# A rebuilt opening for a two-block transformer kernel: x by column halves, the first norm from token rows, weight tiles split one by one

## What is computed

```python
h = rmsnorm(x, norm1[l])        # x*rsqrt(mean(x*x)+1e-6) * gain
proj = h @ w_in[l]              # 1024 -> N_IN; q, k, v of two mixers and the gates
```

## Time and profile before

| | |
|---|---|
| runs, median (lowest to highest) | 2931.31 us (2926.85 to 2935.4) |
| the profiled execution: its time, its span | 2937.29 us, 2935.5 us |
| PE matmul busy | 2825.1 us (96% of the span) |
| PE weight loads busy | 2310.7 us (79%) |
| DVE busy | 1600.3 us (55%) |
| ACT busy | 1122.4 us (38%) |
| POOL busy | 33.6 us (1%) |
| mean granted TensorE clock | 0.984 of 2.4 GHz |
| HBM traffic | 85 GB/s over the span |

### The profile page before, as it was taken

The page is one execution under the profiler, slowest core; times in us unless marked ns, Lnnn a source line. Parts: engine busy times, 40 slices in busy tenths (PEclk is TensorE's granted clock), DMA queues, the critical chain, the costliest instruction groups (busy, mean ns, idle before and its releaser), DMA issues.

```text
span 2935.5 us, 34699 instructions
## 1 busy us (share of the span) xinstructions
PE 2825.1 (96%) x13232; PEld 2310.7 (79%) x13232; DVE 1600.3 (55%) x2164; ACT 1122.4 (38%) x1536; POOL 33.6 (1%) x36
## 2 busy tenths in 40 slices
PE   5999989999999999999999999999999899999998
PEld 4898778888879877788887887888878568788886
DVE  5358665545644866553666655434563445644444
ACT  2126534423412553442343344322442644533222
POOL 2000000000020000000000000000000000000000
PEclk8999999999999999999999999999999999999999
DMA  3322132233322113233324323333232113233322
GB/s 98 105 64 58 58 86 86 86 102 93 106 86 87 44 47 97 72 93 108 96 85 119 91 79 108 93 107 89 86 98 74 29 44 108 65 100 93 102 81 83
DMA packets 467506, 249.91 MB, mean 85 GB/s; under 512 B 21238, under 2 KB 463439, under 8 KB 467279
## 3 DMA queue, kind: packets, MB, share of 16 engines
q1 hardware_dynamic: 467407, 248.54, 29.0%
HBM read 246.41 MB, written 2.10 MB: 85 GB/s over the span
## 4 chain that ended last, share of the span: by engine, by line
PE 88%; DVE 6%; ACT 3%; issue 1%; DMA 1%; SPq 0%; DVEq 0%; ACTq 0%
PE M L655 25%; PE M L656 24%; PE M L657 24%; DVE w_lo L1862 2%; PE M L728 1%; PE M L729 1%; PE M L730 1%; PE A L848 1%; PE A L785 1%; PE A L816 1%; PE A L860 1%; ACT w_hi L1324 1%; PE A L829 0%; PE A L801 0%; PE A L655 0%
## 5 line engine op out<-in xcount | busy, mean ns | idle before, releaser
L655 PE MATMUL M<-h_hi,w_hi 128*128 128x512 f32 x2264 | 893.7, 395 | 10.2 <-DVE w_lo L1862 9.9
L656 PE MATMUL M<-h_lo,w_hi 128*128 128x512 f32 x2264 | 884.2, 391 | 0.0
L657 PE MATMUL M<-h_hi,w_lo 128*128 128x512 f32 x2264 | 884.0, 390 | 0.0
L1324 ACT ACTIVATE w_hi<-stage 128x1024 fp32r<-128x1024 f32 (+3 forms) x516 | 504.3, 1020 | 758.5 <-PE M L657 647.4
L1862 DVE TENSOR_TENSOR w_lo<-stage,w_hi 128x1024 fp32r<-128x1024 f32 (+3 forms) x516 | 610.9, 1222 | 135.7 <-ACT w_hi L1324 134.8
L655 PEld LDWEIGHTS M<-h_hi,w_hi 128*128 128x128 f32 x2264 | 426.7, 188 | 106.1 <-issue 14.4
L656 PEld LDWEIGHTS M<-h_lo,w_hi 128*128 128x128 f32 x2264 | 426.7, 188 | 90.5 <-issue 2.9
L657 PEld LDWEIGHTS M<-h_hi,w_lo 128*128 128x128 f32 x2264 | 426.4, 188 | 89.9
L655 PE MATMUL M<-hid_hi,w_hi 128*128 128x512 f32 x704 | 274.6, 390 | 6.9 <-DVE hid_lo L1996 6.9
L656 PE MATMUL M<-hid_lo,w_hi 128*128 128x512 f32 x704 | 273.9, 389 | 0.0
L657 PE MATMUL M<-hid_hi,w_lo 128*128 128x512 f32 x704 | 273.9, 389 | 0.0
(11 more groups left out here) (417 smaller groups left out, 3351.5 us busy)
## 6 DMA issues: line engine op xcount, KB each, us to landing
stage<-in_w_up SPq DMA_DIRECT2D x88, 512.0 KB, 4.2
stage<-in_ffn_w_gate_up SPq DMA_DIRECT2D x88, 512.0 KB, 3.8
stage<-in_w_in SPq DMA_DIRECT2D x80, 512.0 KB, 3.7
stage<-in_w_down SPq DMA_DIRECT2D x32, 384.0 KB, 3.5
stage<-in_ffn_w_down SPq DMA_DIRECT2D x32, 384.0 KB, 3.5
stage<-in_od_w_in SPq DMA_DIRECT2D x21, 512.0 KB, 3.9
stage<-in_w_down SPq DMA_DIRECT2D x32, 320.0 KB, 3.5
stage<-in_ffn_w_down SPq DMA_DIRECT2D x32, 320.0 KB, 3.3
```

Source lines behind the costliest of these rows:

```text
L655: pe.matmul(bank, a_hi, b_hi, start=(n == 0), stop=False)
L656: pe.matmul(bank, a_hi, b_lo, start=False, stop=False)
L657: last = pe.matmul(bank, a_lo, b_hi, start=False, stop=(n == k - 1))
L1324: act.activation(w_hi[:, s, part * HALF:part * HALF + n], stage[:, part, 0:n], ACT.Copy)\
```

## The change

Line numbers after it are those of the changed kernel. What it does:

- SP's order is now: columns 0 to 511 of x for all tokens (1 MB), the identity (64 KB), `norm1` (16 rows), weight tile 0, columns 512 to 1023 of x (1 MB), weight tile 1, the rest of row group 0, then tile 2 when `w_lo_done` is 1, group 1, tile 3 when it is 2, the other constants, groups 2 and 3 and the gate bias.
- PE turns tile 0, `norm1` alone (L909, into M[1]), tiles 1 to 3, waits for the second half of x, and turns 4 to 7. The tiles go to six banks (`turn_bank`), so only tiles 6 and 7 wait for a bank.
- ACT and DVE make `h_hi` (L1620) and `h_lo` (L2257) directly from the turned banks; DVE copies them to `x` (L2262) in between.
- The four tiles of chunks 0 and 1 are split one by one (L1615, L2251); PE takes a tile (24 matmuls, L681 to L683) when that tile is split.
- The sum of squares comes from ACT over token rows (`Square` with accumulation, L1631), 4 of 128x1024; `rstd_col` is made from it (L1634, L1636), and PE spreads it to `rstd` by 4 transposes (L934) after chunk 0, which ACT copies (L1639). DVE's 8 additions and PE's sums are gone.
- The rest of `vec` is turned after chunk 1 (L946) and read after DVE has split chunk 3 (L2305).

```diff
-            sp.dma_start(const[:, 0:C_BIAS], dram["shape_constants"][:, 0:C_BIAS]).then_inc(tokens_landed, 16)
-            for j in range(TT):
-                sp.dma_start(x_tok[:, j, :], dram["x"][0, j * P:(j + 1) * P, :]).then_inc(tokens_landed, 16)
...
+            sp.dma_start(x_tok[:, :, 0:half], x_rows[:, :, 0:half]).then_inc(tokens_landed, 16)
+            sp.dma_start(const[:, 0:P], dram["shape_constants"][:, 0:P]).then_inc(tokens_landed, 16)
+            sp.dma_start(rows[0:DEPTH * KT, 0, :], dram["norm1"].rearrange("a (r c) -> (a r) c", c=P)).then_inc(tokens_landed, 16)
+            sp.dma_start(halves(KT, P)[0], first[0]).then_inc(landed[0], 16)
+            sp.dma_start(x_tok[:, :, half:D], x_rows[:, :, half:D]).then_inc(rest_landed, 16)
+            sp.dma_start(halves(KT, P)[1], first[1]).then_inc(landed[1], 16)
+            load_rows(0, 1)
+            sp.wait_ge(w_lo_done, 1)
+            sp.dma_start(halves(KT, P)[0], first[2]).then_inc(landed[0], 16)
+            load_rows(1)
+            sp.wait_ge(w_lo_done, 2)
+            sp.dma_start(halves(KT, P)[1], first[3]).then_inc(landed[1], 16)
...
+            def first_projections(c0, n):
+
+                pe.wait_ge(w_lo_done, 1)
+                product(M[0][:, :], weight(0, 0), ready_tiles, KT)
+                pe.wait_ge(w_lo_done, 2)
+                pe.wait_ge(consts_set, 2)
+                product(M[1][:, :], weight(0, 1), normal, KT).then_inc(w_used, 1)
+                pe.wait_ge(root_done, TT + 2)
+                pe.wait_ge(turned_out, KT)
+                for j in range(TT):
+                    last = pe.transpose(A[0][:, j * P:(j + 1) * P], rstd_col[:, j:j + 1].broadcast_to([P, P]), ident)
+                last.then_inc(spread_done, 1)
+                pe.wait_ge(w_lo_done, 3)
+                product(M[2][:, :], weight(1, 0), normal, KT)
+                pe.wait_ge(w_lo_done, 4)
+                product(M[3][:, :], weight(1, 1), normal, KT).then_inc(w_used, 1)
...
-            split_hi(0, 0)
-            split_hi(1, 1)
...
+            turned_hi(0)
+            turned_hi(1)
+            split_hi_part(0, 0, 0)
+            for k in range(2, KT):
+                turned_hi(k)
+            split_hi_part(0, 0, 1)
+            for j in range(TT):
+                act.activation(token_square[:, j, :], x_tok[:, j, :], ACT.Square,
+                               accum_out=rstd_col[:, j:j + 1]).then_inc(root_done, 1)
...
+            split_hi_part(1, 1, 0)
+            act.wait_ge(spread_done, 1)
+            act.activation(rstd[:, :], A[0][:, :], ACT.Copy).then_inc(rstd_done, 1)
+            split_hi_part(1, 1, 1)
...
-            split_lo(0, 0)
-            split_lo(1, 1)
-
-            clear_sum(0)
...
+            turned_lo(0)
+            turned_x(0)
+            turned_lo(1)
+            split_lo_part(0, 0, 0)
+            turned_x(1)
+            for k in range(2, 6):
+                turned_lo(k)
+            for k in (4, 5):
+                turned_x(k)
+            turned_lo(6)
+            turned_lo(7)
+            split_lo_part(0, 0, 1)
+            for k in TURN_ORDER[4:]:
+                turned_x(k)
+            split_lo_part(1, 1, 0)
+            split_lo_part(1, 1, 1)
```

More of the change, by code:

```diff
@@ new lines, in _, with ready_tiles @@
+            turn_tokens(4)
+            turn_tokens(5)
+            for k in (6, 7):
+                pe.wait_ge(turned_out, k - 5)
+                turn_tokens(k)
+            def ready_tiles(k):
+                pe.wait_ge(h_lo_done, k + 1)
+                return h_hi[:, k, :], h_lo[:, k, :]
+            def first_projections(c0, n):
[13 more added lines that the diff above has]
+                product(M[3][:, :], weight(1, 1), normal, KT).then_inc(w_used, 1)
+                pe.wait_ge(rstd_done, 1)
+                pe.wait_ge(inputs_landed, 16 * INPUTS)
+                for r in range(TT):
+                    last = pe.matmul(A[1][:, r:r + 1], by_residue(rstd[0:1, :], 1)[:, r, :], ones[0:1, 0:1], start=True, stop=True)
+                last.then_inc(turned, 1)
+                for g, (at, n_rows) in enumerate(VEC_ROWS):
+                    last = pe.transpose(A[2][:, at:at + n_rows], rows[0:n_rows, g, :], ident[0:n_rows, 0:n_rows])
+                last.then_inc(turned, 1)
+                with pe.Fori(1, n // 2) as i:
+                    for s in range(2):
+                        two_tiles(i * 2 + (c0 + s), s, normal, KT)
```

136 lines of the change are left out of this document (86 added, 50 removed).

## The result

The changed kernel took 2899.49 us (median of four runs, 2896.33 to 2901.61); the kernel before, beside it, 2930.43 us (four runs, 2926.85 to 2935.4). The ratio is 0.9887, 95% interval 0.9875 to 0.9899: 31 us faster by the medians, 30 to 37 by the interval. The forecast was 2909. The time lies inside the range 2898 to 2917, but near its lower end and by the mechanism of rival A, which the range left out; that it lies inside is luck.

What follows compares the result with a forecast made beforehand. PE's matmuls were taken to bound the program, with only the opening to win. Its terms summed to -22.1 us, taking the profiled 2937.3 to 2915.2; set against the median, 2909 us, range 2898 to 2917.

Steps and rivals of the forecast that it cites:

- rival A: In chunk 1 DVE's subtraction slips between two of POOL's casts, so no long stall: gain 36.7, 2895 us; chance 0.07.
- What bounds the kernel and where time lies: Whole program: PE's matmuls carry 88% of the chain; only the opening can win, and the program behind it stays the same.
- The loads and the turning: Opening: loads at 0.347 MB/us, first transpose at 6.1 us, first product at 14.1 instead of 40.4: -26.3 us.
- Chunk 0: First products at full clock take 10.9 us instead of 12.8, ending at 25.0: -1.9 us.
- The clock: Chunk 0: transposes raise PE to full clock before the first product; otherwise a slow start, +2.7 us, ending about 27.7.
- Chunk 1, the term of +14.2: Second low part meets POOL's casts and waits until 43.0; PE stands still 11.6 us, then runs slow: +14.2 us.
- Between chunks 1 and 2: Four small matmuls and 4 transposes between the chunks take 1.8 us instead of 4.7: -2.9 us.
- Chunk 2: Takes 10.9 us instead of 13.9 with its 13 slow matmuls, ending at 64.2: -3.0 us.
- The median from the profile: Whole time: 2915.2 from the profiled run, which lies 6 us above the median of 2931.3, becomes 2909 us.
- B: Chunk 1: both low parts are caught by the casts, chunk 1 running 43.1 to 56.8; gain 16.8, 2914.5 us; chance 0.09.
- C: Opening's short stops keep PE at 1.2 GHz through chunks 0 to 2 and into the fourth: 2940 us or more; chance 0.03.
- D: No gain at the program's end, because some later wait does not move with PE; chance 0.03.

Runs made afterwards that it cites:

- before_late2: Kernel before with half of the fill of v_a (768 columns) moved to right ahead of chunk 2's first low part in both layers: 2934.71 us, ratio 1.0002.
- after_again: The changed kernel, unedited, run and profiled a second time: 2900.37 us, ratio 0.988.
- after_again2: The changed kernel, unedited, run once more in a second session beside after_spread2: 2898.11 us.
- after_spread: The changed kernel with POOL's 16 casts spread, 4 behind the subtractions of each of four chunks: 2897.43 us, ratio 0.9875.
- after_spread2: The same kernel as after_spread, run again in a second session beside the unedited changed kernel: 2898.04 us.
- after_delay3: The changed kernel with a 192-column piece of the fill of v_a ahead of chunk 1's second low part: 2899.41 us, ratio 0.9897.
- after_x_whole: The changed kernel with the second half of x loaded right behind the first, ahead of identity, norm1 and weight tiles: 2899.24 us, ratio 0.9884.
- after_delay2: The changed kernel with a 128-column piece of the fill of v_a ahead of chunk 1's second low part: 2899.99 us, ratio 0.9906.
- after_early_split: The changed kernel with ACT's split of chunk 1's second part moved ahead of the copy of rstd: 2900.44 us, ratio 0.9886.
- after_pair: The changed kernel with PE's first product waiting for both weight tiles of chunk 0: 2908.09 us, ratio 0.9914.
- before_again: The kernel before, unedited, profiled a second time: one run, 2933.6 us.

## Why the prediction was right and wrong

**What bounds the kernel and where time lies**: right. PE's chain, the opening as the one stretch to win, and a program behind it that only shifts (2847.6 us after chunk 2's read, forecast 2849).

**The loads and the turning**: right. First transpose 6.44 (forecast 6.1), first product 13.02 (14.1). The same rate for 2 KB pieces held: the two 1 MB loads landed in 6.3 us. ACT's squares took 1.05 us each, beside 1.09 from rows 11. The first product came 1.1 us early because the later transposes ran at the higher clock: 8 of them from 10.52 took 1.0 us, where the forecast had 0.22 us each. So early, the last 4 did wait for a bank, 0.48 us until DVE's copy of tile 1 was done; the forecast had none.

**Chunk 0**: right, 24.5 for its end (25.0), 11.5 us long (10.9). PE waited 0.3 us for the second tile's low part, made from 17.61 to 18.83, and took it at 18.88. **The clock** was the weighed point. The timeline has the products from 13.33 to 24.27 at 0.39 to 0.40 us each (0.50 once, behind the wait), the duration of the full clock. The transposes again show it, in the rows of L904 from 6 to 9 us and then from 10 to 11 us:

```profile
L904 PE MATMUL A<-const,x_tok x10: 421/421/474, 6.4 to 8.8; 128*128 128x128 f32 x10
```

```profile
L904 PE MATMUL M<-const,x_tok x4: 272/273/407, 10.5 to 11.0; 128*128 128x128 f32 x4
```

Same operation, same size, 421 ns until 10.1 and 273 from 10.8 (407 for the one at 10.52): nothing but transposes ran before, and behind them the clock went from 1.2 to 2.4 GHz. The Trainium skill (TensorE: Matmul & The Clock Gate, Part 4) has transposes not counted as busy; by it chunk 0 would have ended at 27.7. Here the measurement, 24.5, decides against the rule for this kernel's transposes, which the profile records as plain MATMUL.

**Chunk 1, the term of +14.2**: wrong, and this is the step that failed. It measured -0.2. Everything up to it held: the part was made ready behind the copy of `rstd` (forecast 27.8, measured 26.68), POOL had started at 24.73 (25.1), they met, and chunk 1's first part had been made ahead (21.14 to 22.36, forecast about 22.9). What failed is the sentence "So a subtraction of two SBUF operands on DVE stands still until the whole row of casts is over." Two places of one execution, 11 us each, were read as a law, where the runs show two fates with odds of their own: at the place in chunk 1 that the forecast was for, 7 got in and none was shut out, while of the first subtractions of chunk 2 in layer 1, 4 got in and 12 didn't. None of the twelve runs of the changed kernel took more than 2902.88 us, so a stall of 11 us is in none of them. A probability of 0.07 for rival A was far too low for two observations. And the one row beside them, DVE's reads with an operand in PSUM that passed unhindered, told only that the casts don't stop DVE as a whole; it said nothing for a wait of ten casts over a wait of one. The Trainium skill (SBUF — State Buffer, "SBUF: two separate sides") has the lock last one instruction. Where a subtraction got in, that fits: 1.25 to 2.3 us, and POOL's next cast 2.11. Where it was shut out (6.393 us here, 11.284 in rows 7), it doesn't. The page describes one of the two fates.

**Between chunks 1 and 2**: the mechanism right, the size low: 2.4 us where 1.8 stood, since the small matmuls of L943, 8 records for four, took 2.02. **Chunk 2**: -1.3 for -3.0. The clock went to its lower level at the end of those small matmuls. Windows of one us of the changed kernel (length; busy PE, PEld, DVE, ACT, POOL; granted clock; DMA share, GB/s):

```profile
37.00:38.00 1.00, 1.00 (x6) 0.98 (x6) 1.00 (x2) 0.01 (x1) 1.00 (x2) 1.00 1.02 301
38.00:39.00 1.00, 1.00 (x6) 0.90 (x7) 0.09 (x1) 1.00 (x2) 1.00 (x2) 0.52 0.44 130
39.00:40.00 1.00, 1.00 (x4) 0.81 (x3) 0.77 (x1) 0.74 (x2) 1.00 (x2) 0.50 0.01 4
```

From 38.38 to 41.09 six matmuls took 2.71 us where six at full clock take 1.37.

**The median from the profile**: the sum was -22.1 against the profiled run, and the forecast set that against the median of the runs (2931.3). With the right term for chunk 1 the same sum gives -36.5 (its own terms, chunk 1 at -0.2); the profiles lie 36.9 us apart, so the other misses cancel. Set against the median it gives 2895, 4.7 us under what came. That rest isn't in the terms but in taking a sum made from one profile off the median of the runs: the profiled run of before lies 6.9 us above its median (2937.29, 2930.43), that of the changed kernel 0.9. Why is the reading above, argued and not shown: that profile held both shut-outs, a share of which the median run doesn't have.

**Rival A**, with 2895 and "If L2251 has no long one, A is right", is what happened in chunk 1. Its premise doesn't hold: the profile shows no gaps between the casts (24.73, 25.76, 26.82, the first two 1.08 and 1.11 us long). **B, C and D** didn't happen: neither part of chunk 1 was shut out, the longest slow stretch in the opening was 2.7 us, and the gain reached the end of the program nearly whole.

## What to carry to other kernels

A wait of 11 us in a trace is an observation, not a law: when two engines contend, look for the same pair at every place and in several executions, and give both outcomes a price and a chance before the sum is made. A long row of back-to-back GpSimd instructions in front of DVE work that PE waits for is worth breaking up by a wait or two in its program (here 6 us, and a narrower spread of the times), unless, as in layer 0 of the changed kernel, PE has weights in hand when it runs. When the start of a program is idle for its main engine, write ACT's, DVE's and the load queue's order from the first product backward; the order alone gave half of the gain here, and in the changed kernel waiting for one tile in place of two was worth 8 us.

## What the hardware showed that I hadn't expected

- Whether DVE gets in between POOL's casts differs between layers of one execution and between executions of one kernel, with the same 0.62 us of offset into the cast (layers 0 and 1 of `before_late2`). Where it didn't get in at the first or second boundary, it got in at none of the up to nine that were left between casts.
- POOL's cast took 2.07 to 2.22 us in place of 1.08 when a subtraction got in ahead of it: the one that waits can be either engine.
- PE's clock can fall though the records show PE busy all along. It fell to 0.50 at the end of some 2.4 us of matmuls with 1x1 and 112x112 tiles (35.94 to 38.38). That happened in the first profiled execution of the changed kernel and not in the two later ones (`after_again`, `after_again2`); it happened in `after_spread`, `after_spread2`, `after_delay3` and `after_x_whole`, not in `after_delay2`, `after_early_split` and `after_pair`. PE's instructions stand in the same order in all of these. Where it didn't, chunk 2 was read at 49.3 to 49.4, not at 50.8 to 51.0 (53.5 with x whole, 56.8 in `after_pair`, where all lies later). The same window of `after_again` as the second row above:

```profile
38.00:39.00 1.00, 1.00 (x8) 0.87 (x8) 0.05 (x1) 1.00 (x2) 1.00 (x2) 1.00 0.18 52
```

- Transposes of 128x128 in float32, back to back, can raise the clock: from 421 ns to 273 ns each, within 3.2 us of the first in the kernel before (10.29 to 13.51) and within 4.3 in the changed one (6.44 to 10.76). It isn't certain: the second 16 of the kernel before, with short stops between them, took 421 to 476 ns each in the first profile (28.66 to 32.97), and went down to 272 ns in `before_again`.
